# Nine projection products of an attention step in one portion, with values, transposes and scores ahead of them

## The reference

```python
s = einsum('bqhcd,bkhcd->bhcqk', q, k) * ATTN_SCALE      # two maps c = 0, 1 a head, 8 heads
s = where(rel >= 0, s + bias[bucket(rel)], NEG_INF)
p = softmax(s)
w = p[:, :, 0] - lam * p[:, :, 1]
out = einsum('bhqk,bkhe->bqhe', w, v)
o = rmsnorm(out, subln) * (1 - lam_init);  y = o @ w_o
```

## Time and profile before

| | us |
|---|---|
| median of 3 runs | 2788.56 (2787.03 to 2793.2) |
| the profiled execution's own time | 2785.28 |
| its span, first to last instruction | 2783.5 |
| PE busy | 2670.1 (96%) |
| DVE busy | 1426.9 (51%) |
| ACT busy | 684.4 (25%) |
| POOL busy | 839.5 (30%) |
| mean granted TensorE clock | 0.978 of full |

### The profile page before, as it was taken

How to read it: one execution, slowest core, us unless ns; L and a number is a source line. 1 busy time by engine, 2 the same in 40 slices (tenths; PEclk the granted TensorE clock), 3 DMA queues, 4 the chain that set the end, 5 groups by cost and what they waited for, 6 DMA issues and landing times.

```text
span 2783.5 us, 39635 instructions
## 1 busy us (share of the span) xinstructions
PE 2670.1 (96%) x16596; PEld 2586.7 (93%) x16596; DVE 1426.9 (51%) x2220; ACT 684.4 (25%) x1127; POOL 839.5 (30%) x473
## 2 busy tenths in 40 slices
PE   5999999999999999989999999799999999999995
PEld 4999999999999999978888889699999999999995
DVE  6666365444444444474444444536544444444446
ACT  4445131111111111133444444513111111111111
POOL 2342333332333333334333332022333333233231
PEclk8999999999999999989999999899999999999998
DMA  3111311111111111123222222311111111111111
GB/s 131 35 50 31 116 39 45 46 46 46 46 46 46 46 46 46 51 104 122 78 86 86 86 91 79 146 44 46 46 44 42 45 46 46 46 46 46 46 46 69
DMA packets 78672, 170.51 MB, mean 61 GB/s; under 512 B 9333, under 2 KB 44149, under 8 KB 78238
## 3 DMA queue, kind: packets, MB, share of 16 engines
q1 hardware_dynamic: 71442, 140.02, 15.5%
q10 hardware_dynamic: 7052, 27.96, 2.7%
HBM read 145.91 MB, written 26.76 MB: 62 GB/s over the span
## 4 chain that ended last, share of the span: by engine, by line
PE 87%; DVE 7%; ACT 3%; issue 2%; POOL 1%; ACTq 0%; DVEq 0%; POOLq 0%
PE psum L714 69%; PE psum L856 4%; PE psum L860 3%; PE psum L858 3%; PE psum L909 2%; PE psum L885 2%; DVE line L1448 2%; DVE x L1513 2%; PE psum L897 1%; ACT line L1215 1%; PE psum L935 1%; PE psum L961 1%; DVE line L1489 1%; POOL w_lo L606 1%; DVE inverse_rms L1501 0%
## 5 line engine op out<-in xcount | busy, mean ns | idle before, releaser
L714 PE MATMUL psum<-xn_hi,w_hi 128*128 128x352 f32 x3120 | 679.6, 326 | 32.0 <-DVE xn_lo L1495 13.9
L714 PE MATMUL psum<-xn_lo,w_hi 128*128 128x352 f32 x3120 | 675.1, 324 | 0.0
L714 PE MATMUL psum<-xn_hi,w_lo 128*128 128x352 f32 x3120 | 674.0, 324 | 0.0
L602 POOL TENSOR_SCALAR w_hi<-w_raw 128x1024 fp32r<-128x1024 f32 x176 | 189.9, 1079 | 1512.5 <-PE psum L714 1499.5
L714 PEld LDWEIGHTS psum<-xn_hi,w_hi 128*128 128x128 f32 x3120 | 533.8, 190 | 35.9 <-issue 21.9
L714 PEld LDWEIGHTS psum<-xn_lo,w_hi 128*128 128x128 f32 x3120 | 538.1, 189 | 0.0
L714 PEld LDWEIGHTS psum<-xn_hi,w_lo 128*128 128x128 f32 x3120 | 532.1, 188 | 0.0
L606 POOL TENSOR_TENSOR w_lo<-w_raw,w_hi 128x1024 fp32r<-128x1024 f32 x176 | 453.6, 2577 | 14.7
L1215 ACT ACTIVATE line<-line,columns 128x1072 f32<-128x1072 f32 x96 | 123.4, 1285 | 1062.3 <-DVE line L1471 1062.3
L1513 DVE TENSOR_TENSOR x<-psum,x 128x1056 f32<-128x1056 f32 x208 | 261.2, 1256 | 227.7 <-PE psum L714 226.9
L1466 DVE TENSOR_TENSOR line<-psum,inverse_rms 128x704 f32<-128x704 f32 x104 | 92.8, 892 | 472.0 <-PE psum L714 471.9
(11 more groups left out here) (213 smaller groups left out, 2691.4 us busy)
## 6 DMA issues: line engine op xcount, KB each, us to landing
w_raw<-in_w SPq DMA_DIRECT2D x200, 512.0 KB, 3.5
k_pages<-in_cache_k SPq DMA_DIRECT2D x128, 64.0 KB, 1.9
v_pages<-in_cache_v SPq DMA_DIRECT2D x128, 64.0 KB, 1.9
scratch_line<-scratch_row ACTq DMA_DIRECT2D x1, 4608.0 KB, 21.3
x<-in_x ACTq DMA_DIRECT2D x8, 528.0 KB, 10.9
scratch_x<-x ACTq DMA_DIRECT2D x1, 4224.0 KB, 12.1
out_k<-raw ACTq DMA_DIRECT2D x8, 528.0 KB, 3.2
out_v<-raw ACTq DMA_DIRECT2D x8, 528.0 KB, 3.1
```

Source lines behind the costliest of these rows:

```text
L602: pool.tensor_scalar(WHI[:, s], WRAW[:, s], 1.0, 0.0, ALU.mult, ALU.add).then_inc(w_hi, 1)
L714: last = pe.matmul(PS[:, 3 * (a % 2) + c, 0:CH], w[:, s, k, :], r[:, c * CH:(c + 1) * CH], start=start and first, stop=stop and final)
```

## The change

PE's step is put in another order: values of step g - 3, transposes of step g - 2, scores of step g, then all nine products at once, then what comes once a head, each of which moves one step earlier. The ring's order, ACT's and DVE's follow. `square_sum` and `output_rows` lag three steps instead of four. The sample's squares are made within step 62 and their root within step 63, and the last transposes (step 63) move behind the first part of the output projection.

```diff
--- before.py
+++ after.py
@@ -178,17 +178,17 @@
     order = []
     for g in range(STEPS + 3):
         h, t = divmod(g, 8)
+        if g >= 3:
+            order.append(("o", g - 3))
         if 2 <= g < STEPS + 2:
             order += [("w", g - 2, b) for b in range(halves(g - 2))]
-        if g < STEPS and t == 2:
+        if g < STEPS and t == 1:
             order += [("v", h, 0), ("v", h, 1), ("v", h, 2)]
-        if g < STEPS and t in (1, 3, 5):
+        if g < STEPS and t in (0, 2, 4):
             order.append((("scores", "weights", "output")[t // 2], h))
-        if g >= 3:
-            order.append(("o", g - 3))
-        if g < STEPS and h and t >= 6:
-            order.append(("ot", h - 1, t - 6))
-        if g == STEPS:
+        if g < STEPS and h and t in (5, 6):
+            order.append(("ot", h - 1, t - 5))
+        if g == STEPS - 2:
             order.append(("squares",))
     return order + [("ot", NH - 1, 0), ("ot", NH - 1, 1)]
 
@@ -986,36 +986,36 @@
             fill(LEAD)
             for g in range(STEPS):
                 h, t = divmod(g, 8)
-                scores(g)
-                fill(RATE // 3)
+                if g >= 3:
+                    values(g - 3)
                 if g >= 2:
                     turn_weights(g - 2)
+                scores(g)
+                fill(RATE)
+                if t == 0:
+                    sample_scores(h)
+                if t == 1:
+                    turn_values(h)
                 if t == 2:
-                    turn_values(h)
-                fill(RATE // 3)
-                if t == 1:
-                    sample_scores(h)
-                if t == 3:
                     sample_weights(h)
-                if t == 5:
+                if t == 4:
                     sample_output(h)
-                if g >= 3:
-                    values(g - 3)
-                fill(RATE - 2 * (RATE // 3))
-                if h and t >= 6:
-                    turn_output(h - 1, t - 6)
+                if h and t in (5, 6):
+                    turn_output(h - 1, t - 5)
+                if g == STEPS - 2:
+                    pe.wait_ge(sosq_done, 1)
+                    z = open_event("squares")
+                    pe.matmul(PS[:, z, 0:NH * TS], ONES[:, :],
+                              OSQ[:, :, :].rearrange("p h t -> p (h t)"),
+                              start=True, stop=True).then_inc(ev_done, 1)
+            values(STEPS - 3)
             turn_weights(STEPS - 2)
-            values(STEPS - 3)
-            pe.wait_ge(sosq_done, 1)
-            z = open_event("squares")
-            pe.matmul(PS[:, z, 0:NH * TS], ONES[:, :], OSQ[:, :, :].rearrange("p h t -> p (h t)"),
-                      start=True, stop=True).then_inc(ev_done, 1)
-            turn_weights(STEPS - 1)
             pe.wait_ge(raw_done, PRODUCTS // KT)
             pe.wait_ge(ttr_done, 2 * STEPS)
             pe.wait_ge(osl_done, 1)
             project(range(0, 2))
             values(STEPS - 2)
+            turn_weights(STEPS - 1)
             project(range(2, 4))
             values(STEPS - 1)
             project(range(4, NH - 1))
@@ -1374,22 +1374,25 @@
             keys_out(0)
             for g in range(STEPS):
                 h, t = divmod(g, 8)
-                if h and t == 7:
-                    output_back(h - 1, 0)
-                if h > 1 and t == 0:
-                    output_back(h - 2, 1)
-                if t == 4:
+                if h and t >= 6:
+                    output_back(h - 1, t - 6)
+                if g == STEPS - 1:
+                    wait_event(act, "squares")
+                    act.activation(OSQ[:, :, :].rearrange("p h t -> p (h t)"),
+                                   PS[:, bank(("squares",)), 0:NH * TS], ACT.Sqrt, scale=1.0 / P,
+                                   bias=EPSC[:, :]).then_inc(ev_free[EV["squares",] % 2], 1)
+                if t == 3:
                     sample_second(h)
+                if t == 2:
+                    values_out(h)
                 if g >= 2:
                     weights_back(g - 2)
-                if t == 2:
-                    values_out(h)
                 exponentials(g)
-                if t == 2:
+                if t == 1:
                     sample_exponentials(h)
-                if g >= 4:
-                    square_sum(g - 4)
-                if h and t == 4:
+                if g >= 3:
+                    square_sum(g - 3)
+                if h and t == 3:
                     deviation(h - 1)
                 if t == 4 and h + 1 < NH:
                     high_qk(3 * h + 3)
@@ -1399,22 +1402,17 @@
                     keys_out(h + 1)
                 if g >= STEPS - 6:
                     high_o(g - (STEPS - 6))
-                if g == STEPS - 2:
+                if g == STEPS - 3:
                     act.wait_ge(osm_done, 1)
                     act.activation(OSQ[:, :, :], OSM[:, :, :], ACT.Square).then_inc(sosq_done, 1)
-            output_back(NH - 2, 1)
             weights_back(STEPS - 2)
-            square_sum(STEPS - 4)
-            wait_event(act, "squares")
-            act.activation(OSQ[:, :, :].rearrange("p h t -> p (h t)"),
-                           PS[:, bank(("squares",)), 0:NH * TS], ACT.Sqrt,
-                           scale=1.0 / P, bias=EPSC[:, :]).then_inc(ev_free[EV["squares",] % 2], 1)
-            weights_back(STEPS - 1)
             act.wait_ge(son_done, 1)
             act.activation(XNH[:, :, SEQ:T], OSM[:, :, :], ACT.Copy, scale=SUBG[:, :]
                            ).then_inc(osh_done, 1)
             high_o(NH - 2)
-            for g in range(STEPS - 3, STEPS):
+            square_sum(STEPS - 3)
+            weights_back(STEPS - 1)
+            for g in range(STEPS - 2, STEPS):
                 square_sum(g)
             deviation(NH - 1)
             for half in range(2):
@@ -1918,33 +1916,32 @@
 
             for g in range(STEPS):
                 h, t = divmod(g, 8)
-                if g >= 4:
-                    output_rows(g - 4)
-                if t == 2:
+                if t == 1:
                     sample_biased(h)
-                if t == 4:
+                if t == 3:
                     sample_combined(h)
-                if t == 6:
+                if t == 5:
                     sample_rows(h)
+                if g >= 3:
+                    output_rows(g - 3)
                 biased(g)
-                evac_chunks(chunks_by(g, RATE // 3))
+                evac_chunks(chunks_by(g, 0))
                 if g:
                     combine(g - 1)
-                if t == 1:
+                if t == 0:
                     sample_biases(h)
-                if t == 3:
+                if t == 2:
                     sample_normalized(h)
+                if h and t == 3:
+                    variance(h - 1)
                 if h and t == 4:
-                    variance(h - 1)
-                if h and t == 5:
                     scaled(h - 1)
-                if g == STEPS - 2:
+                if g == STEPS - 3:
                     wait_event_read(dve, "output", NH - 1)
                     dve.memset(CARRY[:, 5:6], 0.0).then_inc(osm_done, 1)
-                evac_chunks(chunks_by(g, 2 * (RATE // 3)))
+                evac_chunks(chunks_by(g, RATE // 2 + 1))
                 if g >= STEPS - 6:
                     low_o(g - (STEPS - 6))
-            output_rows(STEPS - 4)
             combine(STEPS - 1)
             output_rows(STEPS - 3)
             wait_event_read(dve, "squares")
```

## The result

| | before | after |
|---|---|---|
| median, us | 2788.16 (4 runs, 2787.03 to 2793.2) | 2835.91 (4 runs, 2833.55 to 2839.12) |
| ratio, 95% interval | 1 | 1.0166 (1.015 to 1.0182) |
| profiled execution, us | 2785.28 | 2836.51 |
| first projection matmul of the loop, us of the span | 1252.26 | 1252.74 |
| first matmul behind the last projection matmul (end of the full part) | 1742.18 | 1773.92 |

The account below looks back on a forecast made before the run. In the full part TensorE's starts sum to the time; the tail has waits. Profiled 2785.28 + 0 grouping + 15.9 waits + 12 tail = 2813.2; with the median 3.3 above the profiled run, 2816 us, range 2793 to 2834.

Parts of the forecast that it names:

- Grouping: Full part, 57 steps: two of three breaks in the projection go, taken as 0 us a step.
- a break pays itself back: Projection breaks: leaving transposes is 0.08 us cheaper, the first projection matmul behind 0.09 dearer, so the pair is nought.
- Turned values: Step 1 to 2 of each head: values wait for ScalarE's second copy of the turned values, 0.50 us.
- sample weights: Step 2 to 3 of each head: transposes wait for the sample weights' readers on ScalarE and VectorE, 0.67 us.
- steps 1 and 5: Second half of a step's transposes waits for the output rows' copy, 0.11 us each, 0.22 a head.
- the chunk: Step 3: a projection chunk waits for VectorE's copy of the chunk before last, behind two bias passes, 0.37 us.
- Second output turn: Step 6 to 7 of each head: TensorE waits for ScalarE's read of the output turn, 0.6 us (0.33 to 0.75).
- a rival at 0.10: Half clock behind the sample output lasts twice as long, another 1.6 us in each of 8 heads: 2829 us, chance 0.10.
- The tail: Last projection matmul to first output-projection matmul: 67.3 us against 55.8, 11.5 more; with last transposes +12 (+4 to +17).
- that of 61: Tail: sample output's reader stands behind step 60's low part (37.2), then transposes and scores; bias pass 61 at 40.9 us.
- Only the tail: Rival: readers are early enough, the full part loses nothing and only the tail's 12 us remain: 2801 us, chance 0.14.
- faster: Rival: breaks cost 0.085 us each, 9.7 us gained in the full part, waits vanish, tail breaks even: 2775 us, chance 0.11.

Follow-up runs that it names:

- experiment 1: The kernel before with the transposes directly behind the scores, so one projection break fewer a step; 2788.62 us beside 2787.56, ratio 0.9995.
- experiment 5: The changed kernel with the second output turn read ahead of the key split and step 4's sample output between products 4 and 5; 2830.09 us, ratio 1.0136.
- experiment 6: The changed kernel with GpSimd's weight split started one chunk (8 products) later in every unit; 2847.99 us, ratio 1.0212.
- Experiment 3: The changed kernel with ScalarE's copy of the second output turn ahead of the key split of step 6 instead of behind it; 2829.0 us, ratio 1.014.
- experiment 9: The kernel before with only the end's edits: squares and root early, last transposes within the output projection; 2786.43 us beside 2787.51, ratio 0.9992.

## Why the prediction fell short

*Grouping, forecast 0.* Right within 3 us. The reason given, that a break pays itself back, isn't borne out by experiment 1, where one break fewer makes a head 0.45 us shorter. In the new order nothing of such a gain is left to see: a head with the short slow stretch takes 70.9 us in experiment 5, and the waits priced below, with 0.4 at the output turn, account for about 2.3 of the 2.4 more. Either way the change could not gain much: what it bought was worth a few us at most.

*Waits priced from durations.* Turned values 0.50 (0.50 forecast), sample weights 0.68 (0.67), steps 1 and 5 0.18 each (0.11 each), the chunk 0.4 (0.37): right to 0.1 us. Durations from the trace of before carried these.

*Second output turn, forecast 0.6 (0.33 to 0.75).* This is the first step that failed: 2.0 us in five heads and 0.4 in the sixth, 6.8 us more than forecast. I had seen that ScalarE does the key split first, and that this waits for the chunk copy behind VectorE's combination, and called it 0.4 us late. The combination of this step takes 3.45 us beside GpSimd (1683.01 to 1686.46), where 1.28 do in experiment 6. The trace before could have told me: there it took 3.0, with nothing waiting for it, since the chunk copy stood ahead of it. The step that failed is thus the lateness of ScalarE's read: an operation off the critical path was priced at its undisturbed length when the change put it on the path. Experiment 3 takes this wait away by the order on ScalarE, experiment 6 by moving GpSimd's work.

*Clock, forecast as one slow stretch a head and a rival at 0.10.* The second failure, a term that the sum left at nothing. At half clock the full part has twelve times 3.41 us after the change and seven before; the five more are three behind the wait of step 7 and two by doubling behind the sample output. A doubled stretch costs 1.6 us (heads of 70.9 and 72.5 in experiment 5), so five are 8 us. With it 15.9 + 6.8 + 8 = 30.7, where 31.3 was measured. The two doubled stretches, 3.2 us of this, are partly the luck of the two traces: the same full part has two of them in experiment 9. My rival had the place but not the cause: it expected values and transposes to keep the clock down in every head, and even with them gone (experiment 5) it stays down in as many. The rule that I weighed for it, that transposes don't count as busy for the clock (the Trainium skill, TensorE: Matmul & The Clock Gate, Part 4: PE-mode transpose), isn't decided by this: in the trace after the change five of seven heads are back at full clock after 3.41 us of values, transposes and scores, two are not.

*The tail, forecast 11.5 and measured 17.2.* The starts held for the first half. Starts of the bias passes behind the last projection matmul, forecast and measured: 57 at 7.1 and 7.3, 58 at 16.5 and 16.7, 59 at 24.5 and 25.9, 60 at 31.9 and 33.4, 61 at 40.9 and 46.0, 62 at 48.5 and 52.8, 63 at 57.3 and 63.1; the output projection at 67.3 and 73.07. That 58 came out right is luck. I had TensorE stand 4.6 us behind the turned values, for ScalarE's copy; it stood 3.1 us ahead of them, for VectorE's last chunk copy, and only 1.0 and 0.2 behind:

```profile
1784.17 1.09 PE L921 MATMUL psum<-ident,raw 128*128 128x128 f32 x8 [3.08 <-DVE raw L1799]
1786.29 0.40 PE L925 MATMUL psum<-ident,raw 128*32 128x128 f32 x1 [1.03 <-ACT v L1292]
```

The step that failed is that of 61: I took the sample output's reader as the last thing there, and missed that the sample output itself has to wait for a ring bank. The three longest waits of TensorE in the tail behind that of the output projection's first matmul name it, and VectorE's order of time shows why:

```profile
PE psum L957 <- DVE o_q L1811: 3.5, 1, 3.5
PE psum L897 <- ACT o_t_head L1342: 3.2, 1, 3.2
PE psum L944 <- DVE sample_probs L1889: 3.2, 1, 3.2
```

```profile
1805.91 1.23 DVE L1914 TENSOR_TENSOR xn_lo<-xn_lo,xn_hi 128x1024 fp32r<-128x1024 f32 x1 [2.84 <-ACT xn_hi L1368]
1807.06 0.28 DVE L1811 COPY o_q<-psum 128x128 f32<-128x128 f32 x1
```

The output rows are read behind the low part of another head, and the sample output starts at 1807.48 at half clock, where its 34 matmuls take 7.38 us against 3.94. From there the layout is 4 to 6 us late throughout. That the root is done early gave what I counted, 8.9 us down to 4.8 between the low part's end and the output projection; in the old order, by the trace of experiment 9, 8.9 down to 5.6.

*The rivals.* "Only the tail" and "faster" fell with the first rows. Of the forecast's signs in the full part the waits appeared: the values behind ScalarE's copy, the transposes behind VectorE's memset and behind the output copy, a portion of 4.4 us. The 4.6 us behind the turned values of the tail did not, nor did the head of 70.9 us in the kernel after (72.5 to 75.5). It is the one that experiment 5 shows once the output turn is read first and the slow stretch is short. My range was too narrow because it had one price for each wait and no room for two errors of one sign.

## What to carry to other kernels

Where one engine is busy all the time, putting its long filler in one piece saves little (here at most a few tenths of a us a head, none of it left at the end) and takes the cover from one side of every hand-over; ask for each piece how long its input takes (what must lie ahead of it) as well as how long its reader takes (what must lie behind). When work is moved behind an operation, look up what that very operation took in its step, not what its kind takes undisturbed: VectorE's two-input ones beside GpSimd's were already slow in the old trace, where nothing waited for them. Look too at which operations fall beside each other anew, as the variance did. And a wait of 2 us on TensorE can cost more than itself: behind three of five of them the clock fell for 3.41 us, and where experiment 3 took the wait away it didn't.

## What the runs showed of the hardware

- A VectorE operation with two SBUF inputs can stand still until GpSimd's operation beside it has ended: 128x1 1.52 us for 0.22, 128x8 2.33 us for 0.16, 128x768 1.90 us for 1.02. The 128x1 and 128x8 ones end 0.01 to 0.02 us behind GpSimd's, so what they lose is what GpSimd's has left, whatever their own size.
- 34 small matmuls of 4 to 32 columns take 3.94 us at full clock and 7.38 at half, so they scale with the clock though hardly any columns pass.
- Whether the slow stretch behind them is 3.41 or 6.83 us goes with the moment, counted from their start, at which the clock falls, not with the matmuls that follow (76 heads, without exception; the cause is open).
